# Two-block transformer on one core: the second attention layer of the second block computed key group by key group

## The chip, the cores and the metric

One core of one Trainium2 chip runs the whole program in one launch. The metric is the device time of an execution in microseconds (us), lower is better; the runs of the kernel before had a median of 1122.04 us.

## The reference, cut to what matters

One sequence of 256 tokens, width 1024, float32. A first block (two attention branches, a feed-forward network of 4096) is followed by a second block of two layers. Each layer is normalisation, attention, a projection with residual, normalisation, a gated feed-forward network of 2816. The last layer's attention is `nsa_mixer`:

```python
proj = h @ w_in                       # queries 1024 columns, 6 x 128 of keys and values, 48 gates
kc = compress(k_cmp, ...); vc = compress(v_cmp, ...)   # 15 blocks of 32 tokens: flat @ w1, gelu, @ w2
p_c = softmax(q . kc + bias)          # compressed branch, 15 keys
o_cmp = p_c . vc
o_slc = selected blocks               # at 256 tokens every block is selected: full causal attention
o_win = banded_attention(window 512)  # full causal attention too, with other keys and values
o = gates[0] * o_cmp + gates[1] * o_slc + gates[2] * o_win
return o @ w_o
```

There are 16 heads of 64 in two key groups (g = 0 and 1) of 8 heads, which share keys and values.

## The kernel before

**Numbers in halves.** TensorE multiplies in a 4-byte format of reduced precision, so every factor is kept as a high and a low half, and each product is three matmuls (lines 599 to 601 in `mm3`: high by high, high by low, low by high). Weights stream from HBM in slots (`weight_slots`, line 109 on): SyncE loads slot s into one of 4 `raw` buffers once the low halves of slot s-4 are made. A slot is cut into tiles. For tile n ScalarE makes the high half (`split_high`, line 1208; it waits until tile n-4 has been used), then VectorE the low half (`split_low`, line 1757), into rings of 4. `prefetch(n)` in either engine's program makes all halves up to n that are not made yet; `tile(n)` does `prefetch(n + 3)` and waits until TensorE is through with tile n. A full tile of the attention weights has 8 x 3 matmuls of 256 columns (`projected`), a tile of the compressor's first matrix 4 x 3 (`compressor(i)`, i = 0 to 7), and a tile of half the output projection 4 x 3 (`first_half(fc)`, `square_projection`).

**Units.** Attention is cut into units of one branch, one key group and 128 queries (t = 0: 128 keys, t = 1: 256 keys; the compressed branch 15). A unit u passes four times over the engines, in four groups of two heads k = 0 to 3: `scores(u)` on TensorE (lines 823, 824: two matmuls per head, with the high and low half of the keys, into banks 2 to 5), `soften(u)` on VectorE (line 2044: bias and row minimum, then a read of the accumulator), `exps(u, k)` on ScalarE (line 1383, two exps and two reads of the sum), `transposes(u)` on TensorE (line 839, banks 6 and 7), `take_transposed(u, k)` on ScalarE (line 1397), `values(u)` on TensorE (line 851, bank 1) and `finish(u)` on VectorE (line 2065 on: reciprocal, gate, then line 2077 the product and line 2082 the sum over branches in `y_acc`). After the compressed unit of a group and query half, `rows_to_columns(u)` (TensorE, line 865, bank 0), `take_columns(u)` (ScalarE, line 1423) and `y_low(u)` (VectorE, line 2092) make the halves `yh`, `yl` that the output projection multiplies. Its first half (`first_half(fc)`, fc = 0 to 7) needs only the rows of group 0; `add_half(fc, b)` on VectorE (line 2279) adds bank b to the residual `x`, and starts with `prefetch(ST["wo1"] + fc + 4)`. A bank is opened again only when the reader of its last content is through (`open_bank`).

**Order of the work.** Nothing is planned by a program: each engine's queue is written out by hand, strictly in order, in four functions (`block.tensor`, `block.scalar`, `block.vector`, `block.sync`); GpSimd loads bias tables and later sums squares. In the last layer (the `else` branches from line 1033 in TensorE's program, 1574 in ScalarE's, 2315 in VectorE's) the order before is: first keys, values and queries of group 0; then units 8, 9 (selected, g = 0), 10, 11 (window, g = 0), 12, 13, 14, 15 (the same for g = 1), with the projections of group 1's queries `nq4` to `nq7`, of the compressor's inputs `kcmp`, `vcmp` and the eight compressor tiles between; then the GELU, second compressor matrix (`ck`, `cv`), and units 16, 17 (compressed, g = 0), 18, 19 (compressed, g = 1). The TensorE queue before ends like this:

```python
transposes(18, (0, 1)); rows_to_columns(17); transposes(18, (2, 3)); values(18)
first_half(0, 2)
transposes(19, (0, 1)); first_half(1, 3); rows_to_columns(18); transposes(19, (2, 3))
first_half(2, 4)
values(19)
for fc in range(3, 7):
    first_half(fc, 2 + fc % 3)
rows_to_columns(19); first_half(7, 3)
```

The second argument of `first_half` is the bank. After it `square_projection("wo1")` multiplies the second half and waits for `y_low(19)`.

```python
def first_half(fc, b):
    m = ST[f"wo{layer}"] + fc
    tile_ready(m)                                  # low half of tile m is made
    open_bank(b, (x_part, KC * layer + fc + 1))    # next user of b waits for add_half(fc)
    feature_tile(m, half(b), yh, yl, ...)
def add_half(fc, b):
    prefetch(ST[f"wo{layer}"] + fc + 4)
    dve.wait_ge(tiles_done, ST[f"wo{layer}"] + fc + 1)
    dve.tensor_tensor(x[:, fc, :], half(b), x[:, fc, :], ALU.add).then_inc(x_part, 1)
```

## Time and profile before

| | |
|---|---|
| median of 3 runs | 1122.04 us (1120.72 to 1123.84) |
| the profiled execution | 1125.53 us, its span in the trace 1123.7 us, mean TensorE clock 0.964 |
| busy in the span | PE 94%, PEld 92%, DVE 62%, ACT 50%, POOL 17% |
| chain that ended last | PE 79%, DVE 10%, ACT 6%, issue 3%, DMA 1%, POOL 1% |
| TensorE clock in 40 slices of 28 us, tenths | 9888988999999998999999999999995699999999 |
| weights and other loads | 161 MB, 144 GB/s on the mean |

PE is TensorE's matmuls, PEld its weight loads, DVE is VectorE, ACT ScalarE, POOL GpSimd, SP SyncE. The stage of the last layer's attention lies in slices 28 to 32. Matmuls overlap, so a busy PE is not necessarily at its peak.

### The profile page before, as it was taken

Reading aid. Unit: us, or ns where it says so; the run is one execution under the profiler, and the core shown is the slowest. Engines: PE = TensorE matmul, PEld = TensorE weight load, DVE = VectorE, ACT = ScalarE, POOL = GpSimd, SP = SyncE. Lnnn points to the kernel's source line nnn. Section 1 sums busy time; section 2 is a strip of 40 time slices with the busy share of each in tenths; the row PEclk is TensorE's granted clock in tenths of the full one; section 3 lists DMA queues with packets and bytes.
Section 4 is the critical chain, followed back from the end, with each engine's and each line's share of the span. In section 5 each row is a group of like instructions: output and inputs, shape, how many; then the busy total and the mean of one; then the engine's idle time right before and its main releaser. Section 6 shows DMA issues by size and latency. Waiting matters only on the chain.

```text
span 1123.7 us, 23378 instructions
## 1 busy us (share of the span) xinstructions
PE 1060.7 (94%) x8760; PEld 1031.3 (92%) x8760; DVE 702.2 (62%) x1367; ACT 566.1 (50%) x1106; POOL 187.7 (17%) x209
## 2 busy tenths in 40 slices
PE   5888988999999998999999999999999999999997
PEld 5778888999999998899999999999988889999997
DVE  5478664777775445867666664477663486666643
ACT  4354456455664334685544453357773364444431
POOL 5000000053341212002111114210000021111330
PEclk9888999999999999999999999999995699999999
DMA  9432332354555557413666657672151056665741
GB/s 279 84 98 94 114 112 75 116 186 151 187 187 196 180 186 186 151 39 89 174 182 178 180 168 201 183 199 66 57 169 38 4 150 185 186 187 152 211 124 39
DMA packets 221509, 161.40 MB, mean 144 GB/s; under 512 B 7380, under 2 KB 214585, under 8 KB 221435
## 3 DMA queue, kind: packets, MB, share of 16 engines
q1 hardware_dynamic: 218496, 154.23, 45.6%
q0 software_dynamic: 2544, 6.04, 3.2%
q8 instruction: 48, 0.79, 0.3%
q14 instruction: 27, 0.21, 0.1%
q10 hardware_dynamic: 394, 0.13, 0.1%
HBM read 158.28 MB, written 2.10 MB: 143 GB/s over the span
## 4 chain that ended last, share of the span: by engine, by line
PE 79%; DVE 10%; ACT 6%; issue 3%; DMA 1%; POOL 1%; SPq 0%; DVEq 0%; ACTq 0%; POOLq 0%
PE bank L599 23%; PE bank L601 22%; PE bank L600 22%; PE bank L851 4%; DVE w_lo L1757 3%; PE bank L839 2%; PE bank L824 1%; ACT work L1383 1%; ACT w_hi L1208 1%; PE bank L823 1%; DMA raw<-w_in_in 1%; DVE big L1814 1%; PE bank L751 1%; ACT big L1397 1%; DVE steps L1831 1%
## 5 line engine op out<-in xcount | busy, mean ns | idle before, releaser
L1757 DVE TENSOR_TENSOR w_lo<-raw,w_hi 128x1024 fp32r<-128x1024 f32 (+2 forms) x297 | 362.8, 1224 | 235.8 <-ACT w_hi L1208 233.5
L599 PE MATMUL bank<-hh,w_hi 128*128 128x256 f32 x1384 | 398.8, 288 | 15.9 <-ACT work L1354 8.1
L600 PE MATMUL bank<-hl,w_hi 128*128 128x256 f32 x1384 | 394.8, 285 | 0.0
L601 PE MATMUL bank<-hh,w_lo 128*128 128x256 f32 x1384 | 394.8, 285 | 0.0
L1208 ACT ACTIVATE w_hi<-raw 128x1024 fp32r<-128x1024 f32 (+2 forms) x297 | 302.0, 1032 | 173.3 <-PE bank L601 168.4
L599 PEld LDWEIGHTS bank<-hh,w_hi 128*128 128x128 f32 x1384 | 267.4, 193 | 20.9 <-issue 14.1
L600 PEld LDWEIGHTS bank<-hl,w_hi 128*128 128x128 f32 x1384 | 267.8, 194 | 0.1
L601 PEld LDWEIGHTS bank<-hh,w_lo 128*128 128x128 f32 x1384 | 267.5, 193 | 0.1
L599 PE MATMUL bank<-hidh,w_hi 128*128 128x256 f32 x672 | 190.6, 284 | 1.0 <-POOL hidl L2503 1.0
L600 PE MATMUL bank<-hidl,w_hi 128*128 128x256 f32 x672 | 190.2, 283 | 0.0
L601 PE MATMUL bank<-hidh,w_lo 128*128 128x256 f32 x672 | 190.1, 283 | 0.0
L2503 POOL TENSOR_TENSOR hidl<-work,hidh 128x256 f32 (+1 forms) x76 | 82.9, 1091 | 289.2 <-ACT hidh L1471 289.2
L599 PEld LDWEIGHTS bank<-hidh,w_hi 128*128 128x128 f32 x672 | 129.0, 192 | 1.6 <-DVE w_lo L1757 1.3
L600 PEld LDWEIGHTS bank<-hidl,w_hi 128*128 128x128 f32 x672 | 129.0, 192 | 0.0
L601 PEld LDWEIGHTS bank<-hidh,w_lo 128*128 128x128 f32 x672 | 129.0, 192 | 0.0
L2530 POOL MEMSET big<- 128x256 f32 x6 | 1.9, 312 | 457.8 <-DVE x L2138 346.4
L1383 ACT ACTIVATE work<-work,mn 128x256 f32<-128x256 f32 (+2 forms) x160 | 65.8, 416 | 18.0 <-DVE mn L2044 17.8
L1471 ACT ACTIVATE hidh<-work 128x256 f32 (+1 forms) x76 | 31.8, 419 | 71.9 <-DVE work L2211 69.0
L851 PE MATMUL bank<-work,big 128*128 128x64 f32 (+1 forms) x448 | 61.7, 299 | 0.6 <-ACT big L1397 0.6
L851 PEld LDWEIGHTS bank<-work,big 128*128 128x128 f32 (+1 forms) x448 | 60.1, 216 | 1.9 <-ACT big L1397 1.0
L599 PE MATMUL bank<-yh,w_hi 128*128 128x256 f32 x192 | 56.8, 296 | 4.8 <-DVE yl L2092 2.4
L600 PE MATMUL bank<-yl,w_hi 128*128 128x256 f32 x192 | 55.1, 287 | 0.0
(263 smaller groups left out, 1283.3 us busy)
## 6 DMA issues: line engine op xcount, KB each, us to landing
raw<-ffn_w_gu_in SPq DMA_DIRECT2D x88, 512.0 KB, 4.7
raw<-w_ff_in SPq DMA_DIRECT2D x64, 512.0 KB, 4.2
raw<-w_in_in SPq DMA_DIRECT2D x26, 512.0 KB, 6.0
raw<-ffn_w_down_in SPq DMA_DIRECT2D x32, 384.0 KB, 4.2
raw<-ffn_w_down_in SPq DMA_DIRECT2D x32, 320.0 KB, 3.4
raw<-b_w_in_in SPq DMA_DIRECT2D x14, 512.0 KB, 4.8
raw<-a_w_qkv_in SPq DMA_DIRECT2D x10, 512.0 KB, 4.9
raw<-w_out_in SPq DMA_DIRECT2D x8, 512.0 KB, 4.5
```

The lines of the kernel that those rows point to most:

```text
L599: pe.matmul(o, ah, bh, start=start, stop=False)
L600: pe.matmul(o, ah, bl, start=False, stop=False)
L601: return pe.matmul(o, al, bh, start=False, stop=stop)
L751: mm = pe.matmul(o, steps[t][0:rows, g, :], rhs4p[i][0:rows, 0:width // 8, :], start=(i == 0), stop=(i == 2))
L823: pe.matmul(s_full(u, k)[:, j, :], U["q"](h), U["k"](h)[0], start=True, stop=False)
L839: mm = pe.transpose(o[:, j, c, :], s_buf[u % 2][:, h, rows * c:rows * c + rows], ident[:, :])
L851: mm = pe.matmul(psum[V_BANK][:, HD * h:HD * h + HD], PT[0:rows, h, c, :], U["v"](h, c), start=(c == 0), stop=(c == C - 1))
L1208: act.activation(tile_view(w_hi, n), raw_view(n), ACT.Copy).then_inc(hi_done, 1)
L1383: ins = act.activation(s, s, ACT.Exp, scale=-1.0, bias=mn[:, u % 3, h:h + 1], accum_out=ssum[:, u % 3, h:h + 1])
L1471: act.activation(hidh[:, bass.ds(local, 1), :], v_buf[:, (j if name == "ff1" else j // 2) % 2, :].unsqueeze(1), ACT.Copy).then_inc(v_hi, 1)
L1757: dve.tensor_tensor(tile_view(w_lo, n), raw_view(n), tile_view(w_hi, n).bitcast(F32), ALU.subtract)\
L2503: pool.tensor_tensor(hidl[:, bass.ds(local, 1), :], v_buf[:, j % 2, :].unsqueeze(1), hidh[:, bass.ds(local, 1), :].bitcast(F32), ALU.subtr ...
```

## The change

The units are numbered anew: g = 0 has 8, 9 (selected), 10, 11 (window) and now 12, 13 (compressed); g = 1 has 14 to 17 and 18, 19 (compressed). The weight slots are loaded in the new order: the compressor's inputs (columns 1024) as slot 5, then the eight compressor tiles, then the queries of group 1 (tiles n + 19 to n + 22). These queries are projected behind the compressor, into banks 2 to 5, with the GELU between them. The units of group 1 follow, with `first_half` tiles between them, tiles 0 to 5 in bank 0. `y_acc` is shared by both groups. Cut to its core, diff of `weight_slots`, `UNITS` and TensorE's queue:

```diff
-            for c0, width in ((0, 256), (256, 256), (1280, 256), (1792, 48), (1536, 256), (512, 256), (768, 256), (1024, 256)):
+            for c0, width in ((0, 256), (256, 256), (1280, 256), (1792, 48), (1536, 256), (1024, 256)):
...
+            begin("nsa_queries")
+            for c0 in (512, 768):
+                plain("b_w_in_2", 0, 0, KC, c0, 256)
...
-        for g in range(2):
             for t in range(NT):
                 UNITS.append(dict(name="cmp", t=t, nk=NC, scale=HD ** -0.5, branch=0, g=g, first=False, y=4 * g,
...
-                    projected(9, 0, "nq4")
+                    projected(9, 0, "kcmp")
...
+                    transposes(8, (0, 1))
+                    projected(10, 0, "vcmp")
+                    transposes(8, (2, 3))
+                    scores(10)
+                    values(8)
+                    transposes(9, (0, 1))
+                    compressor(0)
+                    transposes(9, (2, 3))
+                    scores(11)
+                    values(9)
+                    compressor(1)
+                    compressor(2)
                     transposes(10, (0, 1))
+                    compressor(3)
                     transposes(10, (2, 3))
                     values(10)
+                    compressor(4)
+                    compressor(5)
                     transposes(11, (0, 1))
+                    compressor(6)
                     transposes(11, (2, 3))
                     values(11)
+                    compressor(7)
+                    projected(19, 2, "nq4")
                     close_bank(mm, "chid", 0)
+                    projected(20, 3, "nq5")
+                    projected(21, 4, "nq6")
                     close_bank(mm, "cv", 2)
+                    projected(22, 5, "nq7")
+                    scores(12); scores(13)
+                    transposes(12); scores(14); values(12)
+                    transposes(13); scores(15); rows_to_columns(12); values(13)
+                    transposes(14, (0, 1)); rows_to_columns(13); transposes(14, (2, 3)); scores(16); values(14)
+                    transposes(15, (0, 1)); first_half(0, 0); transposes(15, (2, 3)); scores(17); values(15)
+                    first_half(1, 0)
+                    transposes(16); scores(18); first_half(2, 0); values(16)
+                    transposes(17, (0, 1)); first_half(3, 0); transposes(17, (2, 3)); scores(19); values(17)
+                    first_half(4, 0)
+                    transposes(18); first_half(5, 0); values(18)
+                    transposes(19, (0, 1)); rows_to_columns(18); transposes(19, (2, 3)); values(19)
+                    first_half(6, 2); rows_to_columns(19); first_half(7, 3)
```

(Statements are joined by semicolons here to save lines.) ScalarE's queue from exps(12) on (`take` stands for `take_transposed`, `exps` for `exps_behind`), and then VectorE's from soften(12) on:

```diff
+   exps(12, 0, 1, 2, 3)
+   for k in range(4): take(12, k); exps(13, k)
+   for k in range(4): take(13, k); exps(14, k)
+   take_columns(12); take(14, 0); take(14, 1); exps(15, 0); take_columns(13); take(14, 2); take(14, 3); exps(15, 1, 2, 3)
+   take(15, 0); take(15, 1); exps(16, 0); take(15, 2); take(15, 3); prefetch(n + 27); exps(16, 1, 2, 3)
+   take(16, 0); take(16, 1); exps(17, 0); take(16, 2); take(16, 3); prefetch(n + 28); exps(17, 1, 2, 3)
+   take(17, 0); take(17, 1); prefetch(n + 29); exps(18, 0); take(17, 2); take(17, 3); prefetch(n + 30); exps(18, 1, 2, 3)
+   for k in range(4): take(18, k); exps(19, k)
+   prefetch(n + 31); take(19, 0); take(19, 1); prefetch(n + 32); take_columns(18); take(19, 2); take(19, 3)
+   prefetch(n + 33); take_columns(19)
...
+   soften(12); soften(13); prefetch(n + 26); soften(14); finish(12); soften(15); y_low(12); finish(13); y_low(13)
+   soften(16); finish(14); add_half(0, 0); soften(17); finish(15); add_half(1, 0); soften(18); add_half(2, 0)
+   finish(16); add_half(3, 0); soften(19); finish(17); add_half(4, 0); add_half(5, 0); finish(18); y_low(18)
+   finish(19); add_half(6, 2); y_low(19); add_half(7, 3)
```

Here n + 23 is the first tile of the output projection, so n + 27 is what `add_half(0)` asks for. Between scores(8) and the query tiles ScalarE has `compressor_rows`, `compressor_high`, `compressed_rows` and one `prefetch` each behind the groups of exps of units 9 to 11, and VectorE `compressor_positions` and `compressor_low` behind soften(8) to (11).

## Rows read from the trace of the kernel before

**Rows 1.** Stretches (us): us, busy of PE, PEld, DVE, ACT, POOL, PEclk, DMA share, GB/s.

```profile
763.70:834.00 70.30, 68.57 (x592) 66.73 (x591) 49.01 (x178) 53.86 (x170) 0.00 (x0) 1.00 0.32 106
834.00:841.40 7.40, 5.42 (x50) 4.52 (x48) 4.09 (x11) 7.18 (x26) 0.00 (x0) 0.99 0.00 0
841.40:889.10 47.70, 45.85 (x208) 41.49 (x209) 16.17 (x91) 17.71 (x87) 0.00 (x0) 0.50 0.08 23
889.10:902.50 13.40, 12.74 (x107) 12.31 (x105) 9.03 (x18) 5.87 (x11) 0.00 (x0) 1.00 0.29 79
```

**Rows 2.** The same view, around the fall and the rise of the clock.

```profile
840.00:841.00 1.00, 0.00 (x0) 0.00 (x0) 0.41 (x1) 1.00 (x3) 0.00 (x0) 1.00 0.00 0
841.00:842.00 1.00, 0.26 (x2) 0.29 (x3) 0.00 (x0) 1.00 (x4) 0.00 (x0) 0.64 0.00 0
...
888.00:889.00 1.00, 1.00 (x7) 1.00 (x7) 0.66 (x2) 0.07 (x1) 0.00 (x0) 0.50 0.00 0
889.00:890.00 1.00, 1.00 (x10) 1.00 (x10) 0.00 (x0) 0.13 (x1) 0.00 (x0) 0.97 0.00 0
```

**Rows 3.** The chain that ended last, at full clock: start, us, what.

```profile
776.77 1.78 PE bank L851 x16
...
786.13 0.87 PE bank L839 x8
788.92 3.52 PE bank L851 x32
...
890.64 0.12 PE bank L599
...
892.08 1.92 PE bank L851 x16
```

**Rows 4.** The same chain, at half clock.

```profile
843.68 6.72 PE bank L851 x32
...
850.53 0.21 PE bank L824
...
862.84 3.60 PE bank L851 x16
```

**Rows 5.** Groups of instructions by shape, 763.7 to 834: busy us, mean ns | idle before, releasers.

```profile
L1383 ACT ACTIVATE work<-work,mn 128x256 f32<-128x256 f32 x24 | 11.9, 503 | 0.0
L1208 ACT ACTIVATE w_hi<-raw 128x1024 fp32r<-128x1024 f32 x11 | 11.6, 1053 | 1.6 <-PE bank L601 1.6
...
L1590 ACT ACTIVATE work<-bank 64x240 f32<-64x240 f32 x8 | 3.0, 374 | 4.2 <-PE bank L601 4.1
```

**Rows 6.** Waits of PE from 763.7 to 834 (us, times, longest), then its timeline.

```profile
PE bank L839 <- ACT big L1397: 1.1, 1, 1.1
PE bank L599 <- DVE qs L2252: 0.7, 1, 0.7
...
834.71 0.40 PE L1116 MATMUL bank<-ident_sb,work 30*128 30x30 f32 x4
...
838.75 0.42 PE L1127 MATMUL bank<-work,cw 128*64 128x30 f32 x4
839.10 0.62 PE L1132 MATMUL bank<-cw,work 128*15 128x64 f32 x8
```

**Rows 7.** Timeline of ACT, the copies of unit 16, one turn apart.

```profile
857.67 0.37 ACT L1397 ACTIVATE big<-bank 15x256 f32<-15x256 f32 x1 [2.76 <-PE bank L839]
...
858.53 0.36 ACT L1397 ACTIVATE big<-bank 15x256 f32<-15x256 f32 x1
```

**Rows 8.** The chain, ahead of a rows_to_columns.

```profile
876.91 0.70 DVE work L2077
...
877.63 0.70 DVE work L2082
...
878.38 1.11 PE bank L865 x4
```

**Rows 9.** The chain, from a high split to the first tile of the second half.

```profile
900.04 0.64 ACT w_hi L1208
900.70 0.69 DVE w_lo L1757
901.39 0.34 DVE x L2279
901.73 0.61 DVE yl L2092
...
902.47 0.35 PE bank L599
```

**Rows 10.** Stretches elsewhere with small matmuls, columns as in rows 1.

```profile
104.20:107.40 3.20, 2.57 (x98) 2.51 (x97) 2.56 (x4) 0.92 (x3) 0.00 (x0) 1.00 0.98 301
...
489.00:503.40 14.40, 12.98 (x113) 12.45 (x112) 10.53 (x45) 11.14 (x39) 0.00 (x0) 1.00 0.21 60
...
107.00:108.00 1.00, 1.00 (x24) 1.00 (x20) 1.00 (x2) 0.46 (x3) 0.00 (x0) 0.71 0.67 234
```

More of the change, by code:

```diff
@@ L222, in build_program @@
         PT = area(big, 0, HU, 2, P)
-        s9 = ExitStack()
-        y_rows = sb("y_rows", [P, NT, HU, HD], where=s9)
-        s9.close()
         hh = sb("hh", [P, KC, T], F32R)
@@ L341, in build_program @@
         v2 = area(work, 22400, 2, NT, P)
-        y_acc = [[area(work, 12160, HU, HD), area(work, 17792, HU, HD)],
-                 [y_rows[:, t, :, :] for t in range(NT)]]
+        y_acc = [area(work, 12160, HU, HD), area(work, 17792, HU, HD)]
         y_tmp = area(work, 12672, HU, HD)
@@ L1118, in _ @@
                     close_bank(mm, "chid", 0)
-                    transposes(14, (2, 3))
-                    values(14)
-                    transposes(15, (0, 1))
+                    projected(20, 3, "nq5")
+                    projected(21, 4, "nq6")
                     pe.wait_ge(cg, 1)
@@ L1699, in _ @@
                     ins.then_inc(q_hi, 1)
+                    query_high(n + 22, 7, 5)
+                    prefetch(n + 26)
+                    exps_behind(12, 0, 1, 2, 3)
+                    for k in range(4):
+                        take_transposed(12, k)
+                        exps_behind(13, k)
+                    for k in range(4):
+                        take_transposed(13, k)
+                        exps_behind(14, k)
+                    take_columns(12)
+                    take_transposed(14, 0)
@@ L1716, in _ @@
-                    take_transposed(18, 3)
-                    exps_behind(19, 1, 2, 3)
-                    prefetch(ST["wo1"] + 4)
+                    prefetch(n + 27)
+                    exps_behind(16, 1, 2, 3)
+                    take_transposed(16, 0)
+                    take_transposed(16, 1)
+                    exps_behind(17, 0)
+                    take_transposed(16, 2)
+                    take_transposed(16, 3)
+                    prefetch(n + 28)
+                    exps_behind(17, 1, 2, 3)
@@ new lines, in _ @@
+                    take_transposed(17, 0)
+                    take_transposed(17, 1)
+                    prefetch(n + 29)
+                    exps_behind(18, 0)
+                    take_transposed(17, 2)
+                    take_transposed(17, 3)
+                    prefetch(n + 30)
+                    exps_behind(18, 1, 2, 3)
+                    for k in range(4):
+                        take_transposed(18, k)
+                        exps_behind(19, k)
+                    prefetch(n + 31)
@@ L2411, in _ @@
                     dve.tensor_copy(c_v[0:NC, :, :], half(2)[0:NC, 0:2 * HD].rearrange("p (g d) -> p g d", g=2)).then_inc(ev_dve, 1)
+                    query_low(n + 22, 7, 5, 18 + 19)
+                    soften(12)
+                    soften(13)
                     prefetch(n + 26)
+                    soften(14)
+                    finish(12)
+                    soften(15)
+                    y_low(12)
+                    finish(13)
+                    y_low(13)
+                    soften(16)
+                    finish(14)
+                    add_half(0, 0)
+                    soften(17)
                     finish(15)
-                    soften(16)
-                    soften(17)
+                    add_half(1, 0)
                     soften(18)
+                    add_half(2, 0)
                     finish(16)
+                    add_half(3, 0)
                     soften(19)
-                    y_low(16)
                     finish(17)
-                    y_low(17)
+                    add_half(4, 0)
+                    add_half(5, 0)
                     finish(18)
-                    add_half(0, 2)
-                    add_half(1, 3)
                     y_low(18)
-                    add_half(2, 4)
                     finish(19)
-                    for fc in range(3, 7):
-                        add_half(fc, 2 + fc % 3)
+                    add_half(6, 2)
                     y_low(19)
```

200 lines of the change are left out of this document (73 added, 127 removed).

## The prediction

> **What bounds the kernel now.** I read the page first (TensorE is busy 94% of the span, but its clock digits fall to 5 and 6 in two slices), then the stretches of the stage that the diff touches, then the chain and the timelines inside it. The stage runs from scores(8) at 763.7 us to the first matmul of the projection's second half at 902.47. [rows 1] shows three parts. Until 834.0 TensorE is busy 68.6 of 70.3 us at the full clock (2.4 GHz) and bounds. From 834.0 to 841.4 it is busy 5.4 of 7.4 us: the compressor's GELU and the last transposes wait for ScalarE. From 841.4 to 889.1 TensorE is busy nearly throughout, at half clock (1.2 GHz), so these 47.7 us hold about 24 us of work at full clock. [rows 2] puts the fall at about 841.4, after 2 us with hardly a matmul, and the rise at about 889.0, five us into the first output tiles. Between the two stand only transposes, values and narrow scores. DMA moves 8% and less there: it is no bound, and it was 0.32 busy before that.
>
> Durations, full clock [rows 3]: values of a 128-key unit 1.78 us (a compressed unit's the same), of a 256-key unit 3.52; eight transposes 0.87 (so a 256-key unit 1.75, the others 0.9); from 786.13 to 788.92 lie eight transposes and 16 scores of 256 columns, so the scores take 1.95; the others I take at 1.8. One wide matmul is 0.12, an output tile (12) 1.45, a query tile (24) 2.9. Half clock [rows 4]: every matmul starts 0.21 after the last, however narrow, so a score group is 3.45, values 6.9 or 3.6, an output tile 2.56.
>
> **The change, step by step.**
>
> *Up to the last query tile.* Units 12 and 13 (before: 128 and 256 keys of the second group) and scores 14 and 15 no longer stand here: 4.5 + 7.3 + 1.8 + 1.95 = 15.6 us less; the hidden transposes and the compressor's last matmuls now do (0.4 + 1.0 [rows 6]). 834.0 - 15.6 + 1.4 = 819.8. Against that, four units' exps now meet the compressor's work on ScalarE: unit 9 is 8 exps, 4.0 us with what reads the sums [rows 5], and with compressor_rows 1.53 and three splits of 1.05 ScalarE gives values(8), transposes(9), values(10) and values(11) late, by 0.9, 0.7, 1.45 and 1.15 us when I lay the queue out; that is 4.2 us of waits where [rows 6] has 1.8. So 819.8 + 2.4 = 822.2. The GELU (ScalarE and VectorE, some 3.5 us) lies under query tiles 20 and 21, 5.8 us, and costs nothing; without that cover it would cost about what it did, 2 to 4 us. The loads of the moved slots are queued in their new order on SP: each waits for the low split of four slots earlier, and the share of DMA (0.32) leaves room, so 0; the first feed-forward slots are issued near 827 and not at 844, hidden too. POOL's queue has nothing moved. The spared y_rows costs nothing.
>
> *From 822.2 to the end of first_half(1).* Work at full clock: scores 12 and 13 3.5, transposes 12 to 15 4.5, scores 14 to 17 7.5, values 12 to 15 8.9, two rows_to_columns 0.9, two output tiles 2.9: 28.1 us. Waits: transposes(12) alternate with ScalarE's copy and exps, one turn 0.85 us [rows 7], 1.4; transposes(13) 1.1; rows_to_columns(13) for the two VectorE products of finish(13), 1.4 us [rows 8], 1.2. So 31.8, to 854.0.
>
> *first_half(1) to first_half(4).* All output tiles from 0 to 5 go to bank 0, so each waits for add_half of the last, and add_half(k) first makes the low split of tile k+4, whose high split stands in ScalarE's queue behind later exps and copies. The links are in [rows 9]: high 0.64, low 0.69, add 0.34. first_half(2): after tile 1, ScalarE has transposes(16), an exps group of 17, two copies (2.8 us), then high, low, add: 4.6 us, of which TensorE fills 3.1; wait 1.5. first_half(3) waits for the split behind two 256-key copies: 2.5. Behind the waiting add_half on VectorE are soften(18), finish(16) and soften(19), which are not late. Work 15.8, waits 4.4: 20.2 us.
>
> *The tail.* first_half(5) needs add_half(4), whose high split stands behind all of exps(19): four turns of 0.85, then 0.6 + 0.7 + 0.4: it starts 5.75 us after tile 4, with 0.9 of transposes in it. Then rows_to_columns(18) waits for finish(18), which is behind add_half(5) and the split of tile 9: 2.2 + 2.0 = 4.2 us of wait. Further waits: 1.15 inside transposes(18), 0.8 for the copies ahead of values(19), 0.7 for y_low(19) [rows 9]. 10.6 us work, 10.6 waits: 21.2 us. Before, output tiles rotated over three banks, and this hand-back was hidden.
>
> Without any clock change: 854.0 + 20.2 + 21.2 = 895.4, against 902.47: 7 us less.
>
> *The clock.* It cannot be free of falls, I think. [rows 10]: from 104.2 to 107.4 TensorE was busy 2.57 of 3.20 us with 96 matmuls of 16 and 32 columns, and the clock fell at about 107.4; between 489 and 503.4 units of 128 and 256 keys with waits of 0.9 us kept it full. In the new order scores 12 and 13 are 32 matmuls of 30 columns (3.6 us), followed by eight transposes stretched over 2.3: 6 us thinner than the first case. I take the fall at 827.5. It rises where wide matmuls stand together: in [rows 2] one and a half output tiles with 0.85 of transposes between. Here first_half(0) (2.6), transposes 1.7 and scores(17) (3.4, 256 columns) are the next such place, near 862. At half clock scores(14) to scores(17) stretch so that first_half(1) ends at 868.9 and not 854.0: +14.9. In the tail the wait ahead of first_half(5) is 3.7 us without a matmul, longer than the 2 us of [rows 2]: the clock falls again, and tile 5, values 18 and 19, transposes and tile 6 run at half: 28.0 instead of 21.2, until tiles 6 and 7 raise it.
>
> Sum: 868.9 + 20.2 + 28.0 = 917.1; less 902.5: **+14.6 us**. The profiled execution is 1125.53 (span 1123.7), 3.5 above the median of the runs; so 1140 beside it and 1137 beside the median 1122.04. Bounds: the waits at ScalarE before 822 are between 0 and 6 us, the add_half waits between 0 and 15, the clock between 0 and +33.
>
> A rule that speaks here is in the Trainium skill, TensorE: Matmul & The Clock Gate, section HAM oscillation: it is idle waits between bursts that put the clock back. By it alone scores 12 and 13, busy throughout, would not lower the clock, and only the tail would: 902 and a change of 0. The row at 104.2 to 107.4 says otherwise, its idle being 0.6 us. The same page, section PE-mode transpose, says that a transpose doesn't count as busy; by that the pause after scores(13) is emptier still, and transposes(15) between tile 0 and scores(17) would keep the clock down, the long case below.
>
> **Rivals.**
> - *Long half clock.* scores(17) is too short to raise it, and thereafter each output tile stands alone until tiles 6 and 7. values(15) 6.9, tile 1, then 32.8 for 20.2: 936, +33 us. For it: between 843.5 and 850.4 [rows 4] 6.7 us of values at half clock did not raise it. Chance 0.15.
> - *Early rise.* scores(15) alone, 3.4 us of 256 columns at half clock, raises it at 841: first_half(1) ends at 859.4, in all 907.6: +5. Chance 0.20.
> - *Clock falls in the tail only* (the page's rule of idle waits): 854.0 + 20.2 + 28.0 = 902.2: 0. Chance 0.10.
> - *The hand-back of bank 0 is hidden.* If the high splits come early enough (ScalarE is free when the previous tile ends), the waits ahead of tiles 2, 3, 5 and rows_to_columns(18), 12 us, go, and with the 3.7 us pause the second fall: 917.1 - 12 - 6.8 = 898.3, 4 us faster; with no fall at all 884, 18 faster. It decides once those waits shrink below about a third. Against it: the place of prefetch(31) behind exps(19) is written out. Together with no fall and waits as computed (895.4, -7): 0.27.
> - That the reorder does not happen can be excluded: the three queues are rewritten by hand.
>
> **Numbers.** The forecast 0.28, the rivals as given (0.63 of all is slower). 0.3% is 3.4 us, about what this kernel's measurement tells from no change. The likeliest case has 1130 to 1145 for itself. The range reaches from the hidden hand-back, 1113, to 1148: it leaves out the fastest corner (0.08) and most of the long half clock (0.11).
>
> **What would show it.** The clock's slices from 827 on, not 841; then a second drop near 893. A wait of PE for DVE x (add_half) ahead of first_half(2), (3) and (5), and for finish(18) ahead of rows_to_columns(18); no wait at the GELU. The last query tile ends near 822. It is wrong if TensorE shows 2.4 GHz between 827 and 860, if first_half(5) starts within 2 us of transposes(18), or if ScalarE holds values(10) and (11) for more than 3 us each.

## The result, and the profile after

The changed kernel has a median of **1132.87 us** (1130.53, 1132.05, 1133.69 and 1141.08), the kernel before beside it 1121.38: the ratio is 1.0112, with a 95% interval of 1.0058 to 1.0166. That is 11.5 us slower; 1137 was forecast. A ratio here and below is the record's own estimate and not the quotient of the two medians; it leaves out executions more than 1.5% above the fastest of their kernel, which are two of r6_fill_tail's (1138.79 us both). The profiled execution took 1130.53 us, its span 1128.7. The page after: TensorE still 94% busy, and the clock's slices.

```profile
span 1128.7 us, 23378 instructions
PE 1056.9 (94%) x8760; PEld 1026.7 (91%) x8760; DVE 701.1 (62%) x1367; ACT 566.6 (50%) x1106; POOL 187.7 (17%) x209
PEclk9889999999999999999999999999978599999999
```

Before, the low digits were two neighbours, 5 and 6. Now they are three, 7, 8 and 5: the half clock comes in pieces. The stage's ends, first of the kernel before, then of the one after (timelines of PE: the layer's first wide matmul, and after that the first of the projection's second half, whose row for before is in [rows 9]):

```profile
736.37 0.35 PE L599 MATMUL bank<-hh,w_hi 128*128 128x256 f32 x1 [0.32 <-DVE hl L1807]
```

```profile
733.28 0.36 PE L597 MATMUL bank<-hh,w_hi 128*128 128x256 f32 x1 [0.33 <-DVE hl L1804]
...
907.12 0.35 PE L597 MATMUL bank<-yh,w_hi 128*128 128x256 f32 x1
```

The stage took 173.84 us, against 166.10. The rest of the span is alike behind it (221.6 and 221.3 us), and ahead of it this execution happened to be 3.1 us earlier. Its place on the clock, by stretches of the kernel after (columns as in [rows 1]):

```profile
763.70:816.20 52.50, 51.55 (x445) 49.25 (x444) 37.19 (x101) 39.77 (x113) 0.00 (x0) 1.00 0.48 158
816.20:821.00 4.80, 4.24 (x38) 3.82 (x36) 3.37 (x35) 4.29 (x21) 0.00 (x0) 0.99 0.00 0
821.00:834.50 13.50, 12.56 (x56) 10.74 (x57) 5.60 (x29) 7.27 (x39) 0.00 (x0) 0.50 0.29 80
834.50:858.00 23.50, 21.17 (x182) 20.32 (x180) 13.21 (x59) 15.92 (x57) 0.00 (x0) 1.00 0.00 1
858.00:882.00 24.00, 19.54 (x124) 18.41 (x124) 6.89 (x44) 10.06 (x46) 0.00 (x0) 0.79 0.16 45
882.00:907.12 25.12, 18.50 (x84) 16.81 (x85) 7.93 (x17) 4.99 (x14) 0.00 (x0) 0.52 0.00 1
```

What a reader should see: the clock is half from 821 to 834.5, full to 858, mixed to 882, and half to the end of the stage. "Lost to half clock" below means the length of a stretch times one less its PEclk. Here that is 6.8 + 5.0 + 12.1, 23.9 us, and before it was 47.7 x 0.50 = 23.9 as well [rows 1]. This counts idle time too, in which a low clock costs nothing. With TensorE's busy time in place of the length it is about 20 us here and 23 before. So **in this pair of executions the clock does not explain the 7.7 us**: it costs some 3 us less than before, and something else costs more. (The pair is not an average one: 1125.53 us is slow for the kernel before, 1130.53 is the fastest of the changed one. r1_changed below comes back to that.) The waits of PE say what; kernel before from 763.7 to 902.4, then after from 763.7 to 907.1 (total us, times, longest):

```profile
PE bank L839 <- ACT big L1397: 4.0, 6, 2.0
PE bank L599 <- DVE qs L2252: 0.7, 1, 0.7
PE bank L865 <- DVE work L2082: 0.6, 1, 0.6
PE bank L851 <- ACT big L1397: 0.2, 1, 0.2
```

```profile
PE bank L597 <- DVE x L2276: 7.1, 3, 3.5
PE bank L863 <- DVE work L2079: 5.1, 2, 4.1
PE bank L837 <- ACT big L1396: 3.1, 8, 0.5
PE bank L837 <- ACT work L1382: 0.4, 1, 0.4
PE bank L821 <- DVE qs L2249: 0.2, 1, 0.2
```

5.5 us of waits have become 15.9; these 10.4 us, less the 3 of the clock, are about the 7.7. New is the first line, where an output tile (line 597) waits for `add_half` (the addition to x, line 2276), three times; and `rows_to_columns` (line 863; before, line 865), which waited 0.6 us for `finish`, now waits 5.1. Where they stand (timeline of PE, after; the number in brackets is the idle time before):

```profile
858.14 0.36 PE L597 MATMUL bank<-yh,w_hi 128*128 128x256 f32 x1 [1.07 <-DVE x L2276]
866.44 0.36 PE L597 MATMUL bank<-yh,w_hi 128*128 128x256 f32 x1 [2.47 <-DVE x L2276]
884.55 0.55 PE L597 MATMUL bank<-yh,w_hi 128*128 128x256 f32 x1 [3.54 <-DVE x L2276]
896.09 1.11 PE L863 MATMUL bank<-ident_sb,work 128*128 128x128 f32 x4 [4.07 <-DVE work L2079]
```

These are first_half(2), (3), (5) and rows_to_columns(18). The third wait shows what makes them; timeline of ScalarE and VectorE ahead of it:

```profile
881.82 0.36 ACT L1396 ACTIVATE big<-bank 15x256 f32<-15x256 f32 x1
882.09 0.29 ACT L1382 ACTIVATE work<-work,mn 128x15 f32<-128x15 f32 x1
882.38 0.29 ACT L1382 ACTIVATE work<-work,mn 128x15 f32<-128x15 f32 x1
882.66 0.61 ACT L1207 ACTIVATE w_hi<-raw 128x512 fp32r<-128x512 f32 x1
883.38 0.69 DVE L1754 TENSOR_TENSOR w_lo<-raw,w_hi 128x512 fp32r<-128x512 f32 x1 [5.69 <-ACT w_hi L1207]
883.99 0.42 DVE L2276 TENSOR_TENSOR x<-bank,x 128x256 f32<-128x256 f32 x1
```

VectorE stands idle for 5.69 us in `add_half(4)`: for all but the first of them the product it should add is there, but its first statement makes the low half of tile n + 31, whose high half ScalarE makes behind all of exps(19). That half is needed four tiles later. TensorE in turn waits for the addition, because tile 5 goes to the same bank as tile 4.

### The profile page after: what moved, and what is told of

Same layout as the page of the kernel before. It is cut to its first block, busy times and chain, and to the rows that moved or that the text cites. A ratio compares the mean times of both kernels' runs of the same rounds, so it can differ in the third digit from the quotient of the medians.

```text
span 1128.7 us, 23378 instructions
## 1 busy us (share of the span) xinstructions
PE 1056.9 (94%) x8760; PEld 1026.7 (91%) x8760; DVE 701.1 (62%) x1367; ACT 566.6 (50%) x1106; POOL 187.7 (17%) x209
## 4 chain that ended last, share of the span: by engine, by line
PE 77%; DVE 11%; ACT 7%; issue 3%; DMA 1%; POOL 1%; SPq 0%; DVEq 0%; ACTq 0%; POOLq 0%
PE bank L597 22%; PE bank L599 22%; PE bank L598 22%; PE bank L849 4%; DVE w_lo L1754 3%; ACT work L1382 2%; ACT w_hi L1207 2%; PE bank L837 2%; DMA raw<-w_in_in 1%; DVE big L1811 1%; DVE steps L1828 1%; PE bank L822 1%; ACT big L1396 1%; PE bank L821 1%; PE bank L749 1%
## 5 line engine op out<-in xcount | busy, mean ns | idle before, releaser
L597 PE MATMUL bank<-hh,w_hi 128*128 128x256 f32 x1384 | 397.6, 287 | 14.9 <-ACT work L1353 7.5
L1382 ACT ACTIVATE work<-work,mn 128x128 f32<-128x128 f32 (+2 forms) x160 | 66.0, 420 | 10.2 <-DVE mn L2041 10.1
```

Source lines behind the costliest of these rows:

```text
L597: pe.matmul(o, ah, bh, start=start, stop=False)
L1382: ins = act.activation(s, s, ACT.Exp, scale=-1.0, bias=mn[:, u % 3, h:h + 1], accum_out=ssum[:, u % 3, h:h + 1])
```

## The experiments

Each run stands beside runs of the kernel before on the same chip, whose medians were 1121.17 (first four), 1122.84 (next four), 1122.29 (next three) and 1121.61 us (the last). The groups ran on different chips, so runs of different groups are best compared by their ratios. "Lost" is the half clock of the run's own profile between 816 and 925 us, idle time included; it belongs to the profiled execution alone.

| run | median us | ratio to before, 95% | profiled us | lost us |
|---|---|---|---|---|
| r1_changed | 1132.1 | 1.0104 (1.0068 to 1.0140) | 1143.77 | 35.7 |
| r2_early_splits | 1118.12 | 0.9954 (0.9932 to 0.9977) | 1113.22 | 11.9 |
| r3_fill_narrow | 1130.51 | 1.0104 (1.0057 to 1.0151) | 1132.11 | 20.4 |
| r4_tiles_last | 1123.83 | 1.0015 (0.9991 to 1.0038) | 1127.29 | 27.3 |
| r5_add_first | 1118.96 | 0.9973 (0.9944 to 1.0002) | 1113.81 | 11.9 |
| r6_fill_tail | 1125.31 | 1.0046 (1.0010 to 1.0081) | 1125.46 | 15.3 |
| r7_early_but_31 | 1124.75 | 1.0013 (0.9993 to 1.0034) | 1119.85 | 13.6 |
| r8_query_between | 1119.71 | 0.9987 (0.9965 to 1.0008) | 1114.12 | 13.6 |
| r9_tail_order | 1116.51 | 0.9948 (0.9927 to 0.9970) | 1119.84 | 17.0 |
| r10_early_add_tail | 1114.89 | 0.9942 (0.9918 to 0.9967) | 1119.36 | 17.0 |
| r11_dense_fill | 1117.58 | 0.9971 (0.9950 to 0.9992) | 1116.18 | 10.2 |
| r12_short_waits | 1109.70 | 0.9899 (0.9864 to 0.9934) | 1117.31 | 17.0 |

**The changed kernel again.**

> The changed kernel once more, as the yardstick of this group. Measured by the stage (from the first wide matmul of the last layer's projections to the first matmul of square_projection): 166.1 us in the kernel before (736.37 to 902.47), 173.8 in the profiled run of the changed one (733.28 to 907.12). Both theories expect 172 to 182 here, and the time 9 to 15 us above before. If the clock falls at other places from run to run, the number of half-clock stretches differs and the stage with it by 3 us or more.

Its six executions took 1130.67 to 1132.43 (four), 1139.79 and 1143.77 us; the profile is of the last. The waits are those of the first profile of this kernel (6.9 us for x in three, and 1.0 and 4.2 ahead of rows_to_columns). The clock is not; stretches of this run:

```profile
824.00:838.00 14.00, 12.90 (x60) 11.26 (x60) 6.03 (x31) 7.14 (x38) 0.00 (x0) 0.51 0.27 77
...
841.00:855.00 14.00, 13.01 (x63) 12.82 (x62) 4.80 (x22) 7.77 (x27) 0.00 (x0) 0.51 0.00 1
...
868.00:896.00 28.00, 25.20 (x120) 23.45 (x118) 6.25 (x28) 8.32 (x37) 0.00 (x0) 0.51 0.14 39
```

The work of 841 to 855 ran at full clock in the first profile, and that of 868 to 896 (there from about 859 to 881) for about half of it. 35.7 us are lost instead of 23.9, a difference of 11.8 where the two times differ by 13.2. **The queue's waits are the same in both executions; the clock's falls are not.** The changed kernel's ten executions stand in two groups some 10 us apart, and the mean granted clock recorded with each goes with them: 0.962 to 0.967 for the seven from 1130.5 to 1133.7 us, 0.953 to 0.956 for the three from 1139.8 to 1143.8.

These clocks also tell what one pair of profiles cannot. On this chip the spans average 1133.1 us over six executions of the changed kernel and 1119.5 over 23 of the kernel before. Span times one less mean clock is 44.6 and 37.6 us, what remains 1088.5 and 1081.9. (A clock is recorded to three digits, so one product is good to 0.6 us.) So of 13.6 us, 7.0 go with the half clock; some 3 of these are idle time, going by the profiles (about 4 us of what the changed kernel loses, 1 before). **On the average the clock takes about 4 us of the loss and the waits 9 to 10**; that it cost less than before in the first pair was a matter of which two executions were profiled.

**Splits earlier in ScalarE's queue.**

```diff
-   prefetch(n + 28) behind take(16, 3);  prefetch(n + 29) behind take(17, 1);  prefetch(n + 30) behind take(17, 3)
-   prefetch(n + 31) behind exps(19);     prefetch(n + 32) behind take(19, 1)
+   prefetch(n + 28) ahead of take(16, 0); prefetch(n + 29) ahead of take(17, 0); prefetch(n + 30) ahead of take(17, 2)
+   prefetch(n + 31) ahead of take(18, 0); prefetch(n + 32) ahead of take(19, 0)
```

> Only ScalarE's queue differs: each high split of output tiles n+28 to n+32 stands directly behind the point at which its ring place is free, not behind later exps and copies. Theory A (the single bank with add_half behind late splits makes the loss): the waits for DVE x ahead of output tiles 2, 3 and 5 (1.07, 2.47 and 3.54 us) go to below 0.3 each, the wait ahead of rows_to_columns(18) falls from 4.07 to 1.5 to 2; stage 9 to 10 us shorter by these alone, up to 18 with the clock falls that stood in those pauses; the time at or below before. Theory B (the order of units and its effect on the clock makes the loss, the waits only fill time that half clock would take): stage less than 4 us shorter. Theory C (ScalarE's crowding before the queries): stage unchanged or longer, as a split now stands before exps.

Measured: 1118.12 us, 14 us under r1_changed and below the kernel before. Its executions stand in two groups, 1111.7 to 1113.2 and 1118.1 to 1119.8 us; the profile is of the first. Waits of PE from 838 to 908, then stretches of the same run:

```profile
PE bank L863 <- DVE work L2079: 2.5, 2, 1.5
PE bank L837 <- ACT big L1396: 1.9, 3, 0.7
...
```

```profile
823.00:837.00 14.00, 13.07 (x60) 11.26 (x61) 6.03 (x31) 7.25 (x39) 0.00 (x0) 0.51 0.27 77
837.00:881.00 44.00, 39.61 (x339) 37.76 (x339) 24.32 (x109) 28.37 (x110) 0.00 (x0) 1.00 0.09 25
881.00:892.00 11.00, 11.00 (x54) 10.39 (x53) 3.98 (x8) 2.68 (x6) 0.00 (x0) 0.53 0.01 1
```

(The lines left out, here and below, are waits of the second half of the projection and what follows, or of 0.2 us.) The line "<- DVE x L2276" is gone, the wait ahead of rows_to_columns(18) has shrunk from 4.1 to 1.5, and with them the half clock between 838 and 881. No instruction was added or removed: five statements of one queue, placed some microseconds too late, are the slowdown. Over all executions, by the mean clocks as above, the span is 18.9 us shorter than r1_changed's, with 13.6 us less lost and 5.3 us less of the rest. Some 4 us of the 13.6 were idle time, so about 9 us are waits and about 10 the clock: taking out the waits gave back as much again in clock.

**Wide matmuls in the narrow stretch.** 6 extra matmuls of 256 columns behind scores(12), 8 behind scores(13), 4 inside transposes(12); their result is not used.

> 18 wide matmuls of data that nobody reads (128x256, about 2.2 us at full clock) are added between and behind the 30-column scores 12 and 13 and inside transposes(12). Theory A (the narrow scores and the transposes behind them let the clock fall near 821): the granted clock stays at 1.00 from 816 to 835, which gives back 5 to 6 us for 2.2 us of work of which about 1 lies in waits: stage 3 to 5 us shorter. Rival (the fall there has another cause, or comes a little later anyway): clock 0.5 from about 823, stage 1 to 3 us longer.

Measured: 1130.51 us, the ratio equal to r1_changed's. The profile shows the fall at 824 cut to 4 us, a second of 4 us at 834, then 841 to 855 at half clock again. 18 fills cost 2.2 us at full clock, and what they gave back is within the spread. Inconclusive about the price, and r11_dense_fill asks again.

**The new unit order, with the output tiles last.** Units and queries as in the changed kernel; the tiles 0 to 6 stand behind values(18) and rotate over banks 2 to 4, as before the change.

> The new order of the units and of everything up to scores(16), but the output tiles stand at the end in banks 2, 3 and 4, with splits and add_half as in the kernel before. Theory A: no wait for add_half, stage about 11 us shorter than the changed kernel in spite of a half clock from near 855 to the first output tiles: 161 to 166 us, time -5 to 0 against before. Theory B (the order of units makes the loss): stage 170 or more, as the interleaved tiles were what kept the clock up.

Measured: 1123.83 us, the same as before within the interval. All waits for x ahead of the tiles of the first half are gone, but the row 864 to 894 has a PEclk of 0.54 over 30 us: in this profile the units without wide tiles between them run at half clock, as in the kernel before (27.3 us lost). So grouping the units by key group is worth nothing by itself. r2_early_splits, with tiles between the units and the bank handed back in time, has the ratio 0.9954 on the same chip against 1.0015 here, so the tiles between the units are what gives something.

**Addition ahead of the split, in VectorE's queue.**

```diff
 def add_half(fc, b):                       # last layer, fc < 6
-    prefetch(ST["wo1"] + fc + 4)
     dve.wait_ge(tiles_done, ST["wo1"] + fc + 1)
     dve.tensor_tensor(x[:, fc, :], half(b), x[:, fc, :], ALU.add)
+    prefetch(ST["wo1"] + fc + 4)
```

> The changed kernel, with the two statements of add_half(0) to (5) of the last layer swapped: the addition to x first, the low split of tile fc + 4 after it. ScalarE's queue stays as it is. Theory A (a tile waits for the bank, and the bank for an addition that stands behind a split which ScalarE gives late): the three waits ahead of first_half(2), (3) and (5), 7.1 us in all, go or shrink to the time by which the split itself is late for the tile that needs it; the wait ahead of rows_to_columns(18) stays, about 4 us, since finish(18) is still behind the low split of tile n + 32. Kernel 6 to 9 us faster than the changed one, near 1124. Rival B (ScalarE is simply behind, so that moving the split in VectorE's order only moves the wait to the tile's low half or to finish): 0 to 3 us faster, 1129 to 1132, and the trace shows as much waiting under another name (w_lo or work).

Measured: 1118.96 us. No execution took that time: six took 1113.8 to 1115.8 us and six 1122.2 to 1126.3, so the ratios are the better measure (0.9973 against 1.0104, about 15 us under r1_changed). The profile is of the faster group; waits from 838 to 908:

```profile
PE bank L863 <- DVE work L2079: 4.8, 2, 3.8
PE bank L837 <- ACT big L1396: 1.3, 3, 0.5
...
```

Theory A, and more than it asked for: three waits of 7.1 us in all are gone, with ScalarE's queue untouched, and they have not come back under another name. The 3.8 us ahead of rows_to_columns(18) stay, as they should, since finish(18) is still behind the split of tile n + 32. The same split was never needed that early; only its place ahead of the addition made it urgent. Two mends at different ends of one chain give about the same, 15 to 17 us each by the ratios.

**The waits of the tail filled.** 16 matmuls of 256 columns ahead of first_half(5) and 16 ahead of rows_to_columns(18), their result not used.

> The changed kernel with 16 extra matmuls of 256 columns (no result of theirs is used) ahead of first_half(5), and 16 ahead of rows_to_columns(18), in the waits of 3.5 and 4.1 us there. They take 1.9 us each at full clock and 3.8 at half, and so leave the queues' waits as they are. Theory A (in the tail, waits and half clock add up, and the clock falls because of the waits): with the waits filled the clock stays or comes back at full from 885 on, values(18), values(19), tile 5 and tile 6 lose their half clock, 5 to 7 us faster than the changed kernel, 1125 to 1127. Rival B (the narrow values and transposes of units 18 and 19 lower the clock whatever stands between, as the scores and values of units 12 and 13 did): 0 to 2 us faster, and the clock's rows show half clock in the tail as before.

Measured: 1125.31 us, 6.8 under r1_changed (ratio 1.0046 against 1.0104). Eight executions took 1121.5 to 1126.5 us and four 1137.0 to 1138.8; the profile is of the first group. Stretches of the tail:

```profile
883.00:892.00 9.00, 6.78 (x52) 5.82 (x52) 1.03 (x2) 3.73 (x21) 0.00 (x0) 1.00 0.01 2
892.00:896.00 4.00, 3.58 (x16) 3.29 (x16) 2.92 (x7) 0.91 (x3) 0.00 (x0) 0.57 0.00 0
896.00:903.00 7.00, 6.94 (x45) 6.62 (x46) 2.80 (x7) 2.13 (x5) 0.00 (x0) 0.76 0.00 0
```

After had 25.12 us at 0.52 here, this run two pieces with 3.4 us lost. Theory A: of what the tail cost, 6 to 7 us are half clock, over and above the waits themselves (the two profiles differ by 5.9 us from first_half(4) to the second half). The fills both end the pauses and set wide matmuls among narrow ones, so this run alone doesn't tell which of the two holds the clock.

**All splits early but that of tile n + 31.**

> The kernel with the early splits (the second of the first group), but the high split of tile n + 31 stays behind all of exps(19), as in the changed kernel. Theory A (that one place makes the waits ahead of first_half(5) and, through add_half(5), of rows_to_columns(18), and the half clock behind them): the waits of about 3.5 and 4 us are back in the trace and the clock falls in the tail; 6 to 11 us slower than with all splits early, 1124 to 1129; the waits ahead of first_half(2) and (3) stay away. Rival B (what the early splits gave was the first two waits and the clock between 858 and 880): the tail's waits return but cost their own 5 to 6 us only, 1123 or less. Rival C (the order of ScalarE in the tail is bound by exps(19) in any case): under 2 us slower than 1118.

Measured: 1124.75 us, 6.6 over r2_early_splits. Waits from 838 to 908:

```profile
PE bank L597 <- DVE x L2275: 3.5, 1, 3.5
PE bank L863 <- DVE work L2078: 2.4, 2, 1.4
PE bank L837 <- ACT big L1396: 1.6, 3, 0.7
...
```

One statement brings back the one wait of 3.5 us ahead of first_half(5), to the hundredth (3.54), and half clock behind it: theory A in its price. In the two profiles 4.6 us of the difference lie between first_half(4) and the second half, 3.5 of wait and 1.1 of clock; the other 2 stand outside and are not tied to this wait. Wrong in that expectation was the wait ahead of rows_to_columns(18): it stays at 1.4. So the 4.1 us there belong to tile n + 32, whose split stood behind take(19, 1), not to n + 31.

**The last query tile between scores(12) and (13).**

> The kernel with the early splits, and the last query tile, 24 matmuls of 256 columns, placed between scores(12) and scores(13), into bank 0. No work is added. Theory A (the first fall comes from the 4 us of scores with 30 columns that stand in a row, and would come later or be shorter with wide matmuls between them): the fall at 822 to 838, 6.8 us lost, becomes shorter by a half or goes: 3 to 6 us faster than 1118, 1112 to 1115. Rival B (it is the whole thin stretch from scores(12) to scores(15), with transposes and values of 15 keys, that lets the clock fall; the place of one tile in it changes nothing): within 1.5 us of 1118, and the trace shows the fall moved by some us and as much half clock as before.

Measured: 1119.71 us, ratio 0.9987: no gain, rather a loss against r2_early_splits. Stretches:

```profile
816.00:824.00 8.00, 6.79 (x46) 6.47 (x45) 3.00 (x28) 3.86 (x17) 0.00 (x0) 0.79 0.00 1
824.00:838.00 14.00, 12.81 (x59) 10.99 (x60) 6.08 (x30) 7.50 (x40) 0.00 (x0) 0.51 0.28 77
```

Rival B. The clock now drops earlier as well (816 to 824 at 0.79), and the query's copy ahead of three groups of exps makes transposes(12) wait 1.5 us.

**Another order of the tail.** On r2_early_splits: first_half(6) ahead of rows_to_columns(18), first_half(7) ahead of rows_to_columns(19).

> The kernel with the early splits, and in the tail first_half(6) moved ahead of rows_to_columns(18), and first_half(7) ahead of rows_to_columns(19), with the additions and y_low of VectorE in the same order. Theory A (what is left in the tail is the 1.5 us wait for finish(18), in which the clock falls, 5.1 us lost behind it): an output tile of 1.45 us covers it and the clock stays: 4 to 6 us faster than 1118, with a wait of 0.7 us for y_low(19) back ahead of the second half, as the kernel before has it: 1112 to 1115. Rival B (the fall at 881 comes from the 4 us of narrow transposes and values of units 18 and 19, not from the wait): 0 to 1.5 us faster, 1117 to 1118, with the same half clock in the tail.

Measured: 1116.51 us, 1.6 under r2_early_splits (ratio 0.9948 against 0.9954, so within what can be told). Both theories were too simple. The wait of 1.5 us ahead of rows_to_columns(18) is covered and the fall at 881 does not appear (894 to 901 instead, 3.4 us lost), but VectorE now has the split of tile n + 34 ahead of y_low(19), and the first tile of the second half waits 3.0 us for it.

**The three mends together.** r2, r5 and r9 in one kernel.

> The three mends together: splits early in ScalarE's queue, the addition ahead of the split in VectorE's, and the new order in the tail. Theory A: each of the first two mends alone has taken the three waits for the bank away, so together they give nothing over one of them, and this kernel stands within 1 us of the one with early splits and the new tail. Rival B (the one or the other leaves small lateness that a trace does not show as a wait): 1 to 3 us faster than that.

Measured: 1114.89 us; against r9_tail_order the ratios 0.9942 and 0.9948 are equal. Theory A: the early splits and the addition first remove the same waits, so the second adds nothing to the first.

**Dense filling of the narrow stretch.** On r2_early_splits, 48 matmuls of 256 columns between scores(12) and transposes(13), their result not used.

> The kernel with the early splits, with 48 extra matmuls of 256 columns (no result of theirs is used) between scores(12) and values(12): 12 behind each of scores(12) and (13), 8 behind each pair of transposes of unit 12, 8 behind values(12). At full clock they take 5.8 us, of which about 1 us lies in waits. Theory A (narrow matmuls let the clock fall though TensorE is busy; wide ones between them hold it): no half clock between 815 and 845 in the trace, 6.8 us given back for 5 paid, 1115 to 1118. Rival B (the clock falls by something else in this stretch, or the fall only moves to units 13 and 14): half clock of 5 us and more before 860 all the same, 1121 to 1125.

Measured: 1117.58 us. Stretches:

```profile
816.00:839.00 23.00, 21.61 (x178) 19.96 (x177) 11.64 (x76) 12.35 (x61) 0.00 (x0) 1.00 0.17 47
839.00:853.00 14.00, 13.01 (x63) 13.02 (x64) 4.61 (x22) 7.58 (x27) 0.00 (x0) 0.51 0.00 1
```

Every other profile of this order has a fall between 820 and 824, and this one has none. That is theory A's mechanism: those same scores, transposes and values run at full clock when wide matmuls lie between them. The fall at 839, which theory A did not expect, is there all the same. It does not pay: 48 fills cost what they give back (ratio 0.9971, against 0.9954 without them).

**Two waits more taken out.** On r10_early_add_tail:

```diff
 transposes(14, (0, 1))
-rows_to_columns(13)
 transposes(14, (2, 3))
+rows_to_columns(13)
...
-add_half(6, 2); y_low(18); finish(19); add_half(7, 3); y_low(19)        # each add_half with its split ahead
+add_half(6, 2); y_low(18); finish(19); y_low(19); add_half(7, 3)        # no split
+prefetch(n + 34)
```

> The kernel with the three mends, and two waits more taken out of the order: transposes(14) of the pairs 2 and 3 stand ahead of rows_to_columns(13), so that the 1.0 us of finish(13) lies beside them; and in the tail the low splits of tiles n + 33 and n + 34 move behind y_low(19), so that finish(18), finish(19) and y_low(19) no longer stand behind them in VectorE's queue. Theory A (the second fall, at about 839, which about half of the executions show, starts in the pause ahead of rows_to_columns(13), and the 3.0 us ahead of the second half are the split's): the half clock between 839 and 853 becomes rare, the wait for y_low(19) falls from 3.0 to 1.5 us and the one of 1.2 ahead of rows_to_columns(19) goes; median 3 to 5 us under that of the three mends, near 1111, with fewer runs at 1119. Rival B (the second fall comes as often whatever this pause): the tail's 2.7 us only, about 1112, with the two clusters 5 to 6 us apart as before. Rival C (the late splits are then missing at the third tile of the second half, where TensorE waits as long): no change, 1115.

Measured: **1109.70 us**, ratio 0.9899 (0.9864 to 0.9934): 1.0% faster than the kernel before and 22 us under the changed one. Waits from 815 to 925, and the stretch in question:

```profile
PE bank L837 <- ACT big L1396: 3.8, 8, 0.7
PE bank L597 <- DVE yl L2089: 1.6, 1, 1.6
...
```

```profile
838.00:853.00 15.00, 14.59 (x74) 14.35 (x74) 5.34 (x23) 7.91 (x28) 0.00 (x0) 0.54 0.00 1
```

The wait for y_low(19) fell from 3.0 to 1.6, those ahead of rows_to_columns(13), (18) and (19) are gone. But the pause at 839 is gone too, and the clock fell there all the same: in this, rival B. Four of six executions took 1107 to 1110 us (mean clocks 0.977 to 0.982) and two 1117 to 1118 (0.969, the profiled one among them), too few to say whether the second fall has become rarer.

## Why the prediction was right, and where it was not

The sign, the size within 4 us (forecast +15 beside the median before, measured +11.5) and the range from 1113 to 1148 held. The mechanism of the waits held too. The place of the half clock did not, and that the size came so near is in part luck, as told below.

**Right: the mechanism and the waits.** The sum had waits of 1.5, 2.5 and 3.7 us ahead of tiles 2, 3 and 5 and 4.2 ahead of rows_to_columns(18). Measured: 1.07, 2.47, 3.54 and 4.07; r2, r5 and r7 show by three different edits that they come from the places of the splits in the two queues. first_half(1) to first_half(4) was put at 20.2 us with full clock: it took 25.0 with 5.0 us lost, so 20.0. The tail was put at 28.0 with a fall and took 28.4 (from 878.7 to 907.1). In that, two errors cancel: the waits are 8.5 us and not 10.6 (none for y_low(19)), and the clock stays at half to the end of the stage. The 5.75 us to first_half(5) were 5.9 in the trace, but the terms written for them (four turns of 0.85, 0.6, 0.7, 0.4) add up to 5.1 only. "Before, output tiles rotated over three banks, and this hand-back was hidden" holds.

**Wrong in size: the waits for ScalarE up to the last query tile.** The step said 4.2 us; before 816.2 the trace shows 0.5 and 0.4. The layout of ScalarE's queue was too pessimistic. The last query tile ends at 816.2, in the time of the profile before (3.1 later) 819.3, where the prediction had 822.2. The GELU under the query tiles cost nothing, as said.

**Wrong in length: the first half clock.** I took the fall at 827.5 and the rise only at 862, in first_half(0) and scores(17), +14.9 us; in the time of the profile after that is 824 and 859. These rows of after have the fall at 821 and the rise at 834, inside scores(15), which ran from 831.8 to 835.0 with 256 columns:

```profile
820.00:821.00 1.00, 0.64 (x6) 0.32 (x5) 0.85 (x9) 0.98 (x6) 0.00 (x0) 0.97 0.00 0
821.00:822.00 1.00, 0.69 (x3) 0.27 (x4) 0.24 (x1) 1.00 (x8) 0.00 (x0) 0.50 0.03 8
834.00:835.00 1.00, 1.00 (x8) 1.00 (x7) 0.92 (x5) 0.27 (x2) 0.00 (x0) 0.71 0.00 0
835.00:836.00 1.00, 1.00 (x10) 0.83 (x9) 1.00 (x7) 0.34 (x1) 0.00 (x0) 1.00 0.00 0
```

That is the rival "Early rise" (chance 0.20), with 6.8 us lost. The prediction's own sign of being wrong, 2.4 GHz between 827 and 860, is there: from 834.5 to 858 the clock is full. What the forecast had in this one place came in others: 1.7 and 3.4 us between 858 and 879, and in other executions 841 to 855. Forecast: 14.9 + 6.8 = 21.7 us of half clock; measured 23.9 in one profile and 35.7 in the other (20 and 32 by busy time). So the sum of the parts, ends taken in the time of the profile before: 2.9 earlier at the last query tile, 9.2 less to the end of first_half(1) (37.5 against 46.7), 4.8 more to first_half(4), 0.4 more in the tail: 910.2 instead of 917.1, so +7.7 us in this pair where +14.6 was forecast. That execution is the fastest of its four, and the one before a slow one; the forecast 1137 lies between the two groups of executions, 1130.5 to 1133.7 and 1139.8 to 1143.8, and no execution took that time. The median of all came nearer to the forecast than the traced sum did because other falls of the clock, such as those of r1_changed at 841 and 868, stood in for the one that it had misplaced: that is luck. The step that failed is the one that placed the rise: it passed over scores(15) and waited for the first output tile and scores(17). In these rows the clock rose in scores(15), and in r1_changed it rose there too (838) and fell again at 841. (The rival "Long half clock" did not come in either profile; its terms, 868.9 and 4.5 for values(15) and tile 1, 32.8 and 28.0, add up to 934 and not 936.)

**The rule of idle waits.** By the Trainium skill, TensorE: Matmul & The Clock Gate, section HAM oscillation, the waits between bursts put the clock back. r6_fill_tail agrees in the tail: with the waits filled, 3.4 us are lost where 12.1 were, though its fills are wide matmuls besides. It does not cover the first fall, where TensorE was busy 6.42 of the 7 us ahead of it in r2_early_splits, with 30-column scores and narrow transposes; "Clock falls in the tail only" is refuted by the row 821.00:834.50. What a transpose does for the clock, the second point that the prediction takes from that page, no run here shows by itself.

**The hand-back hidden.** The prediction gave 898.3, or 4 us faster, for high splits early enough, with the fall in the tail gone, and said that it decides once the splits come early. r2_early_splits is that case, made on purpose: 3 us under the kernel before. It was the right rival, and the place of five statements decides between the two signs. The size is right in part by chance: its first fall lost 6.8 us and not 14.9, and the tail kept a fall of 5.1 that the rival had gone.

**What stays open.** When the second fall at about 840 comes is not settled. It shows in the profiles of r1, r3, r4, r9, r10, r11 and r12 and not in those of after, r2, r5, r6, r7 and r8, with the same instructions up to there in most of them. Neither the pause there (r12) nor the first fall (r11) decides it. The difference in time seems to go with it: the groups of executions of r9 stand 5 us apart, with mean clocks of 0.974 to 0.976 and of 0.968 to 0.970, and its profile, with the fall, is from the slower group. But of each mended kernel one execution was traced, and r11's profile has the fall and is among its faster ones.

## What to carry to other kernels

A helper that prepares something for four steps later must not stand ahead of the statement that frees a buffer now: put the freeing statement first, or see that what the helper waits for comes early; here the order of two statements on VectorE was worth about 15 us of 1132 (ratio 1.0104 against 0.9973). When tiles are spread between other work through one buffer, list for each hand-back everything that its engine has to do ahead of it, on all queues, since what was hidden by a rotation over three buffers no longer is. And price a wait on a matmul-bound stretch at more than its length: 3.5 us of wait at one place came with 6.6 us of time (r7_early_but_31), of which the profiles show 4.6 in the tail. And do not judge a clock loss from one pair of profiles: average it over executions.

## What the runs showed of the hardware

- TensorE's clock fell to 1.2 GHz here while the engine was busy: in r2_early_splits 6.42 of the 7.00 us ahead of 823, with 30-column scores and transposes of unit 12, and 13.07 of the 14.00 behind it at 0.51. With wide matmuls put between the same instructions, 816 to 839 ran at 1.00 (r11_dense_fill).
- The same program's falls differ from one execution to the next: 841 to 855 at 0.51 in r1_changed, in the first profile of the same kernel at 1.00. In r1, r2, r5, r6 and r9 the times stand in two groups 5 to 14 us apart; the kernel before too is spread from 1117.2 to 1125.7 us on one chip, with mean clocks from 0.972 to 0.962. This makes one profile a poor witness for the size of a clock loss, though a good one for waits: 3.54, 3.54 and 3.54 us ahead of first_half(5) in after, r3 and r7, 3.44 in r1.
- The clock came back in the scores(15) of 256 columns (834 to 835 in after), where before it had stayed at half through the 6.7 us of values that [rows 4] show from 843.68 on.
